# Two lead blocks on the unnormed residual ahead of the attention's projections, and weight splits moved in the attention's passes

## What is computed

```python
x = x + gate2 * ((silu(g_ff) * up_ff) @ w_ffn_out)
x = rmsnorm(x, norm_f_g) * (1 + scale_f) + shift_f      # end of the first block
u = rmsnorm_2(x, g[0])                                  # start of the second
proj = u @ w_in     # fq, fk, fv, ff, nq, kc, vc, ks, vs, kw, vw, ng
log_f = log_sigmoid(ff + b_f)                           # forget gates, 8 columns
gates = sigmoid(ng)                                     # token gates, 24 columns
```

## Time and profile before

| | us |
|---|---|
| median of 3 runs | 1792.05 |
| lowest, highest | 1791.8, 1792.96 |
| profiled execution | 1791.37 |
| its span | 1789.7 |
| PE busy in the span | 1690.9 |
| mean granted clock | 0.968 |

### The profile page before, as it was taken

One profiled execution on the slowest core, in us unless ns is written; L12 is line 12 of the kernel. 1 busy time (PEld: TensorE's weight loads), 2 busy tenths in 40 slices (PEclk: granted clock), 3 DMA queues, 4 the chain that ended last, 5 costly groups with the idle time before them and its releaser, 6 DMA issues.

```text
span 1789.7 us, 22284 instructions
## 1 busy us (share of the span) xinstructions
PE 1690.9 (94%) x8263; PEld 1328.3 (74%) x8263; DVE 915.0 (51%) x1368; ACT 659.7 (37%) x944; POOL 172.4 (10%) x182
## 2 busy tenths in 40 slices
PE   2999889999999989999998999999999899999996
PEld 1657667888888877666667788888887688888885
DVE  6865584553343353656557644444336744444223
ACT  1324334444322252545554444443225333333221
POOL 5001107940000020000000000002000000000000
PEclk9999889999999989999999899999999799999998
DMA  8664054533332232111102222233222032223221
GB/s 287 211 197 165 25 187 156 179 124 102 104 99 97 81 105 72 47 37 43 42 12 83 71 94 94 96 104 114 97 66 77 26 102 96 94 94 117 97 80 47
DMA packets 48730, 179.78 MB, mean 100 GB/s; under 512 B 5984, under 2 KB 6656, under 8 KB 48416
## 3 DMA queue, kind: packets, MB, share of 16 engines
q1 hardware_dynamic: 44896, 166.75, 27.8%
q0 software_dynamic: 2624, 10.59, 2.0%
q10 hardware_dynamic: 1152, 1.66, 0.3%
HBM read 173.56 MB, written 2.10 MB: 98 GB/s over the span
## 4 chain that ended last, share of the span: by engine, by line
PE 66%; issue 23%; DVE 8%; ACT 2%; DMA 1%; POOL 1%; ACTq 0%; DVEq 0%; POOLq 0%; SPq 0%
PE bank L335 15%; PE bank L337 15%; PE bank L336 15%; PE bank L1252 3%; PE bank L1254 2%; PE bank L1253 2%; PE bank L1316 2%; PE bank L1360 2%; PE bank L1336 2%; PE bank L1086 1%; DVE ada_acc L1724 1%; DVE w_lo L274 1%; PE bank L1416 1%; DMA raw<-in_ada_w 1%; PE bank L429 1%
## 5 line engine op out<-in xcount | busy, mean ns | idle before, releaser
L274 DVE TENSOR_TENSOR w_lo<-raw,w_hi 128x1024 fp32r<-128x1024 f32 (+1 forms) x236 | 322.1, 1365 | 622.0 <-ACT w_hi L270 621.8
L335 PE MATMUL bank<-h_hi,w_hi 128*128 128x512 f32 x1232 | 488.0, 396 | 6.1 <-DVE h_lo L534 2.7
L337 PE MATMUL bank<-h_hi,w_lo 128*128 128x512 f32 x1232 | 481.7, 391 | 0.0
L336 PE MATMUL bank<-h_lo,w_hi 128*128 128x512 f32 x1232 | 481.6, 391 | 0.0
L270 ACT ACTIVATE w_hi<-raw 128x1024 fp32r<-128x1024 f32 (+1 forms) x236 | 265.4, 1125 | 550.9 <-PE bank L337 477.1
L335 PEld LDWEIGHTS bank<-h_hi,w_hi 128*128 128x128 f32 x1232 | 232.3, 189 | 65.1 <-issue 7.1
L337 PEld LDWEIGHTS bank<-h_hi,w_lo 128*128 128x128 f32 x1232 | 232.5, 189 | 49.2
L336 PEld LDWEIGHTS bank<-h_lo,w_hi 128*128 128x128 f32 x1232 | 232.5, 189 | 47.5 <-issue 1.0
L335 PE MATMUL bank<-hid_hi,w_hi 128*128 128x512 f32 x528 | 205.6, 389 | 0.0
L336 PE MATMUL bank<-hid_lo,w_hi 128*128 128x512 f32 x528 | 205.4, 389 | 0.0
L337 PE MATMUL bank<-hid_hi,w_lo 128*128 128x512 f32 x528 | 205.4, 389 | 0.0
(11 more groups left out here) (334 smaller groups left out, 1929.7 us busy)
## 6 DMA issues: line engine op xcount, KB each, us to landing
raw<-in_f2i SPq DMA_DIRECT2D x88, 512.0 KB, 3.2
raw<-in_ffi SPq DMA_DIRECT2D x44, 512.0 KB, 3.3
raw<-in_f2o SPq DMA_DIRECT2D x32, 704.0 KB, 4.1
ada_w<-in_ada_w SPq DMA_DIRECT2D x32, 512.0 KB, 4.0
raw<-in_att_w SPq DMA_DIRECT2D x24, 512.0 KB, 3.3
raw<-in_ffo SPq DMA_DIRECT2D x16, 704.0 KB, 4.0
raw<-in_ada_w SPq DMA_DIRECT2D x16, 512.0 KB, 5.0
raw<-in_w_in SPq DMA_DIRECT2D x16, 512.0 KB, 5.3
```

The lines of the kernel that those rows point to most:

```text
L274: nc.vector.tensor_tensor(WL[par][:, 0:kc * P], RAW[s][:, 0:kc * P], WH[par][:, 0:kc * P].bitcast(F32), ALU.subtract).then_inc(wlo, 1)
L335: pe_.matmul(bank[:, :], w_h, hi[:, k0 + k, :], start=start and k == 0, stop=False)
L336: pe_.matmul(bank[:, :], w_h, lo[:, k0 + k, :], start=False, stop=False)
L337: last = pe_.matmul(bank[:, :], w_l, hi[:, k0 + k, :], start=False, stop=stop and k == kc - 1)
```

## The change

- **One block of gates.** Forget gates (rows 0 to 7) and token gates (rows 32 to 55) share one block of weights; att5 has 7 blocks. The first block number is left out (`no_block`); the gates use slot 1, the compressed keys slot 0.
- **Lead blocks.** In ffo0, ACT also writes HH = X times a gain (`renewed`), DVE its low part FLL. Behind the sum of squares PE multiplies the gates and then the compressed keys by these unnormed chunks. Inside the first stand two broadcasts of the first scale (to RB and PS[3]); behind each stand 16 matmuls of two columns that multiply the same weights by the shift (FSH). DVE multiplies the lead banks by the first scale into FQ (`lead_scaled`), and the shift's products are added when the second scale is applied. The cross sums stand between the two lead blocks.
- **Waits.** ACT writes HH of normed chunk k only after step k of the second lead block (f_step).
- **The loop on normed chunks** now runs the compressed values (slot 1) and, three parts behind, the selected keys (slot 0). The split of the former stands inside the loop over the chunks, that of the latter behind it. The gates' transposes stand behind the selected values.
- **POOL** waits for the second lead block before its small loads.
- **Passes.** The low half of block + 2 is made one slot after the bank is emptied, and `stage` runs in slots 13 to 15 of the pass before.

```diff
+        def no_block(n):
+            return isinstance(n, int) and n == N0["att5"]
         def act_step(n, par, s, kc, rnd):
-            split_hi(n, par, s, kc, rnd)
+            if not no_block(n):
+                split_hi(n, par, s, kc, rnd)
         def dve_step(n, par, s, kc, rnd):
-            split_lo(n, par, s, kc)
...
-            stream("att5", att_w, C * P)
-            stream("att6", att_w, C * P, base=8)
+            sp.wait_ge(wlo, N0["att5"] - 3)
+            sp.sem_inc(ld[0], 16)
+            for s in range(1, 4):
+                sp.wait_ge(wlo, N0["att5"] + s - 3)
+                load(s, att_w[s - 1], C * P)
+            stream("att5", att_w, C * P, base=-1, first=1)
+            stream("att6", att_w, C * P, base=7)
...
+            pool.wait_ge(mm, N0["att5"] + 3)
...
-            pe_sum_last(nj["nf"])
-            pe_bcast(nj["nf"])
-            pe_sum_cross(nj["q0"], 0)
+            pe_sum_last(nj["nf"], no_block=True)
...
-            first_two(N0["att5"], O0["att5"] // 2, range(C), nj["q0"].lo,
-                      lambda step: pe_bcast_next(nj["q0"]) if step == 6 else None)
-            lin("att5", 0, 2)
-            lin("att5", 0, 3)
+            def att_part(w, low, k):
+                w_h, w_l = WH[w][:, k * P:(k + 1) * P], WL[w][:, k * P:(k + 1) * P]
+                pe_.matmul(PS[w][:, :], w_h, HH[:, k, :], start=k == 0, stop=False)
+                pe_.matmul(PS[w][:, :], w_h, low[:, k, :], start=False, stop=False)
+                return pe_.matmul(PS[w][:, :], w_l, HH[:, k, :], start=False, stop=k == C - 1)
+            n5, cnt5 = N0["att5"], O0["att5"] // 2
+            for e, w in enumerate((1, 0)):
+                pe_.wait_ge(ev[w], cnt5 + e)
+                pe_.wait_ge(wlo, n5 + e + 2)
+                for k in range(C):
+                    if e == 0:
+                        pe_.wait_ge(f_lo, k + 1)
+                    m = att_part(w, FLL, k)
+                    if e == 1:
+                        m.then_inc(f_step, 1)
+                    if e == 0 and k == 3:
+                        pe_bcast(nj["nf"])
+                        pe_.matmul(PS[3][:, :], ONE[:, :], DG, start=True, stop=True).then_inc(f_rb, 1)
+                if e == 0:
+                    pe_.wait_ge(f_sh, 2)
+                for k in range(C):
+                    for half, w_ in enumerate((WH[w], WL[w])):
+                        m = pe_.matmul(PS[2][:, 2 * e:2 * e + 2], w_[:, k * P:(k + 1) * P], FSH[:, k, :],
...
+                m.then_inc(mm, 1)
+                if e == 0:
+                    pe_sum_cross(nj["q0"], 0)
+            for step in range(C + LAG):
+                if step < C:
+                    if step == 0:
+                        pe_.wait_ge(ev[1], cnt5 + 1)
+                        pe_.wait_ge(wlo, n5 + 4)
+                    pe_.wait_ge(n_lo, nj["q0"].lo + step + 1)
+                    m = att_part(1, HL, step)
+                    if step == C - 1:
+                        m.then_inc(mm, 1)
+                if step >= LAG:
+                    if step == LAG:
+                        pe_.wait_ge(ev[0], cnt5 + 2)
+                        pe_.wait_ge(wlo, n5 + 5)
+                    m = att_part(0, HL, step - LAG)
+                if step == C - 1:
+                    pe_bcast_next(nj["q0"])
+            m.then_inc(mm, 1)
+            lin("att5", 1, 1)
             pe_.wait_ge(a5["ng"], 1)
...
-            lin("att5", 1, 0)
-            lin("att5", 1, 1)
...
+            act.wait_ge(coef, 1)
+            act.activation(FSH[:, :, 0], GS[:, 0, :], ACT.Copy).then_inc(f_sh, 1)
+            act.wait_ge(mod_ready, 10)
+            def renewed(g, t):
+                m, b = 2 * g + t // 2, t // 2
+                if not t % 2:
+                    return
+                if is_last("ffo0", g, t):
+                    act_gated(nj["nf"], "ffo0", m, b, g)
+                    split_hi(N0["att5"] + 1, 1, 1, C, ROUND["att5"], count=2)
+                    act.activation(TMM[:, b:b + 1, :], X[:, m:m + 1, :], ACT.Square, scale=GS[:, 2, m:m + 1]).then_inc(n_sg, 1)
+                else:
+                    act_gated(nj["nf"], "ffo0", m, b, g, 2)
+                act.activation(HH[:, bass.ds(m, 1), :], X[:, bass.ds(m, 1), :], ACT.Copy,
+                               scale=GL[:, bass.ds(m, 1)]).then_inc(f_hi, 1)
+            phase_splits("ffo0", act, act_step, renewed, hold=True)
+            split_hi(N0["att5"] + 2, 0, 2, C, ROUND["att5"])
             for k in range(C):
                 act.wait_ge(n_t, nj["nf"].t + k + 1)
                 act.activation(X[:, k, :], TMP[:, k % 2, :], ACT.Identity, bias=MOD[:, 48 + k:49 + k]).then_inc(xs[0], 1)
+                act.wait_ge(f_step, k + 1)
                 act.activation(HH[:, k, :], TMP[:, k % 2, :], ACT.Identity, bias=GS[:, 0, k:k + 1],
                                scale=vcol("norm_g2", k)).then_inc(n_hi, 1)
+                if k == 0:
+                    act.wait_ge(f_rb, 1)
+                    act.activation(FK[0][:, :], PS[3][:, :], ACT.Copy).then_inc(f_rf, 1)
+                if k == 2:
+                    split_hi(N0["att5"] + 3, 1, 3, C, ROUND["att5"])
+            split_hi(N0["att5"] + 4, 0, 0, C, ROUND["att5"] + 1)
...
+                    if 4 * g + t >= 3:
+                        split_hi(N0["att5"] + 4 * g + t + 2, t % 2, (t + 2) % 4, C, ROUND["att5"] + g + (t >= 2))
...
+            def final_low(m):
+                dve.wait_ge(f_hi, m + 1)
+                dve.scalar_tensor_tensor(FLL[:, bass.ds(m, 1), :], X[:, bass.ds(m, 1), :], GL[:, bass.ds(m, 1)],
+                                         HH[:, bass.ds(m, 1), :].bitcast(F32), ALU.mult, ALU.subtract).then_inc(f_lo, 1)
+            def renewed(g, t):
+                if not t % 2:
+                    return
+                m, last = 2 * g + t // 2, is_last("ffo0", g, t)
+                dve_gated(nj["nf"], "ffo0", (m, N0["ffo0"] + 4 * g + t + 1), t // 2, 40, last=last, crossed=True)
+                if not last:
+                    final_low(m)
+            phase_splits("ffo0", dve, dve_step, renewed, hold=True)
+            dve.wait_ge(ev[1], O0["att5"] // 2)
+            dve_with_shift(C - 1)
+            split_lo(N0["att5"] + 1, 1, 1, C, count=2)
             dve_mean(nj["nf"], D)
-            dve_with_shift(C - 1)
+            dve.sem_inc(ev[0], 1)
+            dve_with_gain(C - 1, 1)
+            final_low(C - 1)
             dve_diag(nj["nf"], D, mean=False)
-            dve_with_gain(C - 1, 1)
-            last_split("ffo0", dve_step)
+            split_lo(N0["att5"] + 2, 0, 2, C)
+            def lead_scaled(e):
+                dve.wait_ge(mm, N0["att5"] + 2 + e)
+                if e == 0:
+                    dve.wait_ge(f_rf, 1)
+                    dve.tensor_tensor(FQ[1][0:64, :], PS[1][0:64, :], FK[0][0:64, :], ALU.mult).then_inc(ev[1], 1)
+                else:
+                    dve.tensor_tensor(FQ[0][:, :], PS[0][:, :], FK[0][:, :], ALU.mult).then_inc(ev[0], 1)
             dve.wait_ge(n_rb, nj["nf"].turn)
             for k in range(C):
                 dve.scalar_tensor_tensor(TMP[:, k % 2, :], X[:, k, :], GS[:, 2, k:k + 1], RB[:, :], ALU.mult,
                                          ALU.mult).then_inc(n_t, 1)
-                if k == 2:
+                if k == 3:
+                    lead_scaled(0)
+                    split_lo(N0["att5"] + 3, 1, 3, C)
+                if k == 5:
                     dve_next_mean(nj["q0"], 0)
-                if k == 4:
+                if k == 7:
                     diag(nj["q0"], 12)
                 if k >= 1:
                     shifted_low(k - 1)
             shifted_low(C - 1)
+            lead_scaled(1)
+            dve.tensor_reduce(FBI[:, :], PS[2][:, 0:4].rearrange("p (t e) -> p t e", e=2), mybir.AxisListType.X,
+                              ALU.add).then_inc(f_bias, 1)
+            split_lo(N0["att5"] + 4, 0, 0, C)
...
                 if (g, t) == (0, 0):
                     dve.wait_ge(rq_ready, 1)
-                    dve.tensor_tensor(LX, bank[0:NH, :], RQ0[0:NH, :], ALU.mult).then_inc(ev[0], 1)
+                    dve.wait_ge(f_bias, 1)
+                    dve.wait_ge(ev[1], O0["att5"] // 2 + 1)
+                    dve.scalar_tensor_tensor(LX, FQ[1][0:NH, :], FBI[0:NH, 0:1], RQ0[0:NH, :], ALU.add,
+                                             ALU.mult).then_inc(f_lx, 1)
+                    dve.scalar_tensor_tensor(NG, FQ[1][32:32 + 3 * NH, :], FBI[32:32 + 3 * NH, 0:1],
+                                             RQ0[32:32 + 3 * NH, :], ALU.add, ALU.mult).then_inc(f_ng, 1)
                     dve.wait_ge(ld_small, 16 * 3)
-                    dve.wait_ge(ev[0], O0["att5"] // 2 + 1)
+                    dve.wait_ge(f_lx, 1)
                     dve.tensor_scalar(LX, LX, BF[:, 0:1], None, ALU.add).then_inc(a5["xf"], 1)
...
-                split_lo(N0["att6"] + j + 2, t % 2, (t + 2) % 4, C)
+            def att_split(j):
```

(14 more changed lines are left out.)

64 lines of the change are left out of this document (41 added, 23 removed).

## The result

| | median of the runs, us | ratio to before, 95% interval | profiled execution | its span | mean granted clock |
|---|---|---|---|---|---|
| before | 1792.05 (1788.23 to 1793.61) | 1 | 1791.37 | 1789.7 | 0.968 |
| after | 1800.53 (1798.38 to 1801.56) | 1.0049 [1.0038, 1.0061] | 1801.56 | 1799.6 | 0.965 |

The change makes the kernel 0.49% slower, about 8.5 us. The forecast of 1800.4 us was met. That it was met so closely is luck. In the profiled executions, for which the sum was made, the change costs 10.2 us (1791.37 to 1801.56), not 8.3: the turn costs 14.5 us, not 11.9, and the passes give back 5.75 us, not 3.6, so these two errors cancel in the main.

A forecast was written before the change was run, and what follows sets the result against it. TensorE (PE) was taken to set the end. Terms +4.7 (turn at full clock), +7.2 (half clock) and -3.6 (passes) gave +8.3 us on 1791.37, 1799.7, hence a median of 1800.4; range 1791 to 1806.

The forecast's parts named there:

- The lead starts at 633.4: Turn into attention: first lead matmul follows ACT's square and the weight split, 6.9 us before PE's first projection of before.
- Serial chain, first low part at 646.2: Turn: lead blocks, shift products and cross sums delay DVE's first low part from 639.09 to 646.2 at full clock.
- Eight chunks to 660.2, split done 662.3, a wait of some 6 us: Turn: selected keys' split stands behind all eight normed chunks, so PE idles near 6 us.
- Gate chain, 8.7 us, a wait of 7: Behind the second broadcast: gates and table loads delay the selected values' split to 678.0; PE idles about 7 us.
- +4.7 us at full clock and +7.2 for the clock: Turn: selected values end at 684.0 against 679.37, plus three resumptions at half clock of 2.4 us each.
- the 8 to 14 that were named: Sign in the trace: the compressor's matmuls start 8 to 14 us later than 679.88.
- POOL's DMAs at about 652, list end about 664: POOL waits for the second lead block before its DMAs; its list ends later, at no cost, with 15 us left.
- Passes, -3.6 (bounds -4.6 and 0): Attention's four passes: moved splits and slope tables remove PE's waits before the compressed scores, saving 2.4 + 1.2 us.
- The clock didn't hold: Rival in the turn: the clock holds, speed returning at once after PE's waits; +1.1 us, 1793.2; chance 0.17.
- the passes did give something: Rival: the passes give nothing because moved splits or tables push another score late; +11.9 us, 1804.0; chance 0.12.
- PE wasn't fed: Rival in the turn: PE stays fed without a gap from 633.4; -9.9 us and -3.6 in passes, 1778.6; chance 0.09.
- no drain: Rival on the gate chain: each table switch costs a drain of 1.38 us more; +2.8 us, 1803.2; chance 0.02.

The follow-up runs named there:

- e3: The changed kernel with the 18 small cross sums moved from ahead of the second lead block to behind it; 1796.24 us, ratio 1.0029 to before.
- e9: The changed kernel with 28 of the 32 two-column products with the shift left out; 1796.52 us, ratio 1.0036 to before.
- e8: The changed kernel with 22 and 28 useless matmuls put into PE's two waits; 1796.24 us, ratio 1.0032 to before.
- e2: The changed kernel with the passes' edits undone, leaving merged gate weights and two lead blocks; 1803.55 us, ratio 1.0069 to before.
- e4: The changed kernel with the selected values' split and the compressed values' bank emptying ahead of the gate chain, the next block's too; 1789.60 us, ratio 0.9996 to before.
- e7: The changed kernel with both the selected values' split ahead of the gate chain and the cross sums behind the second lead block; 1786.78 us, ratio 0.9976 to before.
- e10: The kernel with merged gates, passes' edits and no lead, plus 10 useless matmuls in PE's 2.54 us wait before the broadcast; 1780.99 us, ratio 0.9953 to before.
- e5: The changed kernel without lead blocks, keeping merged gate weights and the passes' edits; 1780.90 us, ratio 0.9946 to before.

## Why the prediction was right, point by point

- **The lead starts at 633.4.** It did at 633.88, of which 0.4 is a later end of ffo0 in that execution. Right. That it starts at half clock was in the sum, as the first of three stretches.
- **Serial chain, first low part at 646.2.** It came at 651.08. The order of what holds what was right: ACT waited 8.29 us for the second lead block's first step, DVE 9.24 for ACT. The 646.2 is at full clock. Ahead of the low part stand two stretches of half clock, in the first lead block (0.6 + 2.3), which the sum had as 2.4, and at the cross sums and behind them (1.8 and the first part of 1.7), which it had only in its bound. So the low part came behind the 646 to 650 that was to show the forecast right. The products with the shift were 0.11 us apart, for 0.12 taken. The Trainium skill (TensorE: Matmul & The Clock Gate, "Back-to-back issue gap") gives about 81 ns for pairs of load and matmul with 128 columns; 0.11 us is more than that, with two columns.
- **Eight chunks to 660.2, split done 662.3, a wait of some 6 us.** From the first low part's start to the last one's end it took 13.7 us (12.1 + 1.9 expected), split done at 666.6, a wait of 5.76. Right but for the start.
- **Gate chain, 8.7 us, a wait of 7.** From 675.75 to 684.65 it is 8.9, and the wait 7.54. Right, with one term left out: the block also needs the bank of the compressed values, and that is emptied behind the split, 0.69 us later. The Trainium skill (ScalarE: Activation LUTs, "What ACT_TABLE_LOAD costs") gives a drain of about 1.38 us beside each load. None was seen: Exp at 679.87 stands directly behind its load of 1.28 us, as in the earlier trace rows.
- **+4.7 us at full clock and +7.2 for the clock.** Measured at the split behind the selected values: 693.71 against 679.37, less the 0.4 from ahead of the turn, is +13.9, and +14.5 at att6's first matmul. The compressor's first matmul is 14.9 us later (694.80), just over the 8 to 14 that were named. By the windows 10.8 us are clock, which is above the bound of 10.1. This term is mis-sized: there are four stretches, not three. By an estimate from the starts of the matmuls, against the same ones at full clock in e3 and e9, 8.6 us of it lie on the path to the end of the turn, for 7.2: 2.7 in the first lead block, 1.0 in the cross sums, 0.6 in the first step of the second lead block, and 1.7 and 2.6 behind the waits (e8). The other steps of the second lead block lose 1.5 us, which ACT and DVE hide. The second miss is the 0.69 for the bank. What is left of the 2.6 us was not assigned.
- **POOL's DMAs at about 652, list end about 664.** They were issued at 661.42, because the second power, which stands ahead of the new wait, itself waited 24.60 us for DVE's sum. The list ended at 673.1. The wait that the change adds never held anything. There was no cost, as forecast, since the compressor's first matmul came only at 694.80, but the cause and the times were others.
- **Passes, -3.6 (bounds -4.6 and 0).** The edits give -4.26 us by e2 and after. The last wait of 1.55 vanished wholly (1.2 of it was taken), and the profiled executions of before and e2 differ by a further 1.49 of clock. The trace of before held that stretch, and I didn't look at the clock behind that wait. By the timing it is 3.6 us (2.0 to 5.2).
- **Rivals.** The clock didn't hold, the passes did give something, PE wasn't fed, no drain. That the order of queues is what starves PE is shown by e4 for the second wait; for the first no run changes the order alone. The claim that an unstarved lead would reach 1778.6 is not: e7, with the second wait gone and 5.22 us left of the first, is at 1786.8, and the kernel without a lead is better than each with one.

What stays open: what brings the half clock at the second lead block, and whether two leads could pay if the selected keys' weight had a slot of its own. That would need a third slot for split weights, and wasn't tried.

## What to carry to other kernels

Work that is brought forward to fill a wait is worth at most the waits that it can fill; add up the waits of the engine in that stretch first (here 4.6 us for a block of 5.4), and look at which buffer it holds meanwhile, since here the high parts, held by the lead, delayed the chain that set the end. When an engine's order is changed, ask for each weight split behind a long chain (here sigmoid, Exp and Ln with table loads) which block needs it: moving that split ahead, together with the emptying of a bank, was worth 9.5 us in the timing. And a forecast that meets the median within 0.2 us can hide two errors of over 2 us in one execution's trace, and differences of 1 us between a median and the profiled execution: the parts are to be measured apart.

## What the runs showed of the hardware

- Half clock can come while PE is busy: in the fillers of e10 (0.40 us each), behind 16 one-column sums with a wait of 0.72 us among them; inside a row of 34 small products (after: the granted clock falls from 1.00 to 0.50 between 645 and 647) and right behind one of 20 (e9, 643.4). The row of 34 was not followed by it in e3 (653.12).
- What the half clock in the first lead block costs differs by 1.1 us (after and e7 against e3 and e9), with nothing changed ahead of it. In e3, e4 and e9 the block starts at full clock and falls to half behind 3 or 4 matmuls.
- The same wait of 1.55 us at the same place was followed by half clock in the profiled execution of before and by full clock in that of e2. A length read from a single profiled execution can so be off by 1.5 us.
- At half clock 16 one-column sums took 3.55 us (before, e5), at full clock 1.93 (e3, e9, e10); in after, where the clock fell among them, 2.94.
